# First attention of a two-block transformer: mask by a product on the scores, and the log of failure as a maximum

## What is computed

```
def stick_breaking_attention(q, k, v):
    scale = 1.0 / math.sqrt(d)
    for i in range(S // BLOCK):
        t0 = i * BLOCK
        kl = t0 + BLOCK
        z = jnp.einsum('bthd,bshd->bhts', q[:, t0:kl], k[:, :kl]).astype(jnp.float32) * scale
        mask = s_idx < t_idx
        log_fail = jnp.where(mask, jax.nn.log_sigmoid(-z), 0.0)
        later = lax.cumsum(log_fail, axis=3, reverse=True) - log_fail
        a = jnp.where(mask, jnp.exp(jax.nn.log_sigmoid(z) + later), 0.0)
        outs.append(jnp.einsum('bhts,bshd->bthd', a.astype(v.dtype), v[:, :kl]))
```

## Time and profile before

| | |
|---|---|
| median of 3 runs | 1379.29 us (1377.45 to 1379.47) |
| the profiled execution | 1380.28 us, its span 1378.5 us |
| PE matmul busy | 1083.2 us (79% of the span) |
| DVE busy | 480.4 us (35%) |
| ACT busy | 281.4 us (20%) |
| POOL busy | 56.9 us (4%) |
| DMA | 487.14 MB, 353 GB/s over the span |

### The profile page before, as it was taken

The page is one execution under the profiler, slowest core; times in us unless marked ns, Lnnn a source line. Parts: engine busy times, 40 slices in busy tenths (PEclk is TensorE's granted clock), DMA queues, the critical chain, the costliest instruction groups (busy, mean ns, idle before and its releaser), DMA issues.

```text
span 1378.5 us, 16712 instructions
## 1 busy us (share of the span) xinstructions
PE 1083.2 (79%) x7252; PEld 626.7 (45%) x7252; DVE 480.4 (35%) x900; ACT 281.4 (20%) x482; POOL 56.9 (4%) x83
## 2 busy tenths in 40 slices
PE   8999999999999997667684767667666675766766
PEld 7977886799977733132131312313133131312313
DVE  5977777897887311011010110101011010110113
ACT  6536665654254200000000000000000000000001
POOL 0005300000000000000000000000000000000000
PEclk9999999999999998787778887877787878888787
DMA  9755159444435999999999999999999999999995
GB/s 374 277 210 203 62 221 368 166 153 184 184 123 243 382 419 435 430 429 435 429 429 432 432 431 433 426 431 433 429 432 432 429 432 430 430 433 431 429 427 227
DMA packets 24672, 487.14 MB, mean 353 GB/s; under 512 B 2871, under 2 KB 4440, under 8 KB 5784
## 3 DMA queue, kind: packets, MB, share of 16 engines
q1 hardware_dynamic: 23480, 484.51, 83.6%
q10 hardware_dynamic: 1120, 1.57, 0.3%
HBM read 485.02 MB, written 1.05 MB: 353 GB/s over the span
## 4 chain that ended last, share of the span: by engine, by line
PE 68%; another core or an unknown queue 17%; DVE 8%; DMA 4%; issue 2%; ACT 1%; POOL 1%; DVEq 0%; SPq 0%; ACTq 0%
PE ps L284 66%; DMA pair<-in_expert_w 3%; DVE xT L1780 2%; DVE R L1748 1%; DVE R L1744 1%; DVE ring_r L338 1%; PE ps L1788 0%; DVE sm L1399 0%; DMA ring<-in_pieces 0%; POOL hT L796 0%; POOL hT L798 0%; DVE U_r L541 0%; PE ps L1422 0%; DVE hT L1413 0%
## 5 line engine op out<-in xcount | busy, mean ns | idle before, releaser
L284 PE MATMUL ps<-pair,R 128*32 128x512 f32 (+2 forms) x3168 | 485.5, 774 | 245.4 <-DMA pair<-in_expert_w 243.4
L284 PEld LDWEIGHTS ps<-pair,R 128*32 128x32 f32 x3168 | 116.2, 139 | 594.6 <-DMA pair<-in_expert_w 297.6
L284 PE MATMUL ps<-hT_r,ring_r 128*128 128x256 f32 x400 | 113.1, 283 | 0.0
L284 PE MATMUL ps<-U_r,ring_r 128*128 128x256 f32 x480 | 107.7, 284 | 0.4 <-DVE hT_r L529 0.3
L338 DVE TENSOR_TENSOR ring_r<-ring,ring_r 128x2048 fp32r<-128x2048 f32 (+1 forms) x44 | 98.7, 2275 | 23.8 <-ACT ring_r L332 23.6
L1744 DVE SCALAR_TENSOR_TENSOR R<-R,ps 128x512 f32<-128x512 f32 x16 | 11.0, 687 | 271.2 <-PE ps L284 271.2
L1741 DVE SCALAR_TENSOR_TENSOR R<-R,ps 128x512 f32<-128x512 f32 x16 | 11.0, 687 | 265.7 <-ACT R L1736 265.7
L284 PE MATMUL ps<-late_r,ring_r 128*128 128x256 f32 x448 | 84.4, 286 | 1.2 <-DVE U_r L541 0.9
L332 ACT ACTIVATE ring_r<-ring 128x2048 fp32r<-128x2048 f32 (+1 forms) x44 | 81.7, 1896 | 5.7 <-DMA ring<-in_pieces 5.7
L284 PEld LDWEIGHTS ps<-U_r,ring_r 128*128 128x128 f32 x480 | 82.1, 192 | 1.2 <-DVE hT_r L529 1.0
L1795 ACT ACTIVATE R<-ps 128x256 f32<-128x256 f32 x16 | 6.1, 383 | 363.5 <-PE ps L1788 363.5
(11 more groups left out here) (344 smaller groups left out, 1093.2 us busy)
## 6 DMA issues: line engine op xcount, KB each, us to landing
pair<-in_expert_w SPq DMA_DIRECT2D x87, 4096.0 KB, 52.8
ring<-in_pieces SPq DMA_DIRECT2D x20, 2048.0 KB, 8.4
pair<-in_expert_w SPq DMA_DIRECT2D x17, 2048.0 KB, 11.6
ring<-in_wmodt SPq DMA_DIRECT2D x8, 2048.0 KB, 8.2
ring<-in_wmodk SPq DMA_DIRECT2D x4, 2048.0 KB, 8.7
ring<-in_pieces SPq DMA_DIRECT2D x2, 1024.0 KB, 6.7
pair<-in_expert_w SPq DMA_DIRECT2D x2, 1024.0 KB, 41.9
ring<-in_pieces SPq DMA_DIRECT2D x1, 1792.0 KB, 11.8
```

What stands on the lines that cost most here:

```text
L284: mm = lambda e, o, l, r, st, sp_=True, sk=False: e.matmul(o, l, r, start=st, stop=sp_, skip_group_check=sk)
```

## The change

The mask is added to the scores by a product of `identb` with a bfloat16 tile `capb` (0 or -1e30), into the two diagonal pieces of the bank, right behind the scores. With the bank masked, L is worked out as max(z, ln(1 + exp(min(z, 30)))) in `sb_L`; DVE does the minimum and the maximum, ACT the exp and ln as before. The last exponential reads the bank directly. `pool_sb_z` and `dve_sb_c` are gone, and POOL has no part in the attention. `identb`, `causb` and the two halves of `capb` are filled by ACT before the attention, ahead of `act_filters(10)`. In DVE's loop `dve_sb_L` of pair i-1 stands behind `dve_sb_z` of pair i.

```diff
     def pe_sb_z(e, i):
         if i >= 3:
-            e.wait_ge(s["sb_min"], 2 * i - 4)
+            e.wait_ge(s["sb_a"], 2 * i - 4)
         elif i == 0:
             e.wait_ge(s["hf_a"], 7)
             e.wait_ge(s["rms_rt"], ROOTS[1])
+            e.wait_ge(s["b16"], 4)
...
         for h in hs:
-            k = mm(e, sb_b(h)[:, 256:384], k_[h][:, 128:256], q[h][:, 128:256], False, True, True)
+            mm(e, sb_b(h)[:, 256:384], k_[h][:, 128:256], q[h][:, 128:256], False, True, True)
+        for h in hs:
+            k = mm(e, sb_b(h)[:, 0:384].rearrange("p (a t) -> p a t", a=3)[:, 0:3:2, :], identb, capb, False, True, True)
         k.then_inc(s["sb_z"], 1)
 
     def dve_sb_z(e, h):
         e.wait_ge(s["sb_z"], h // 2 + 1)
+        if h >= 4:
+            e.wait_ge(s["sb_L"], h - 3)
+        elif h == 2:
+            e.wait_ge(s["gate"], 4)
+        e.tensor_scalar(sb_e1(h), sb_b(h)[:, 0:384], 30.0, None, ALU.min).then_inc(s["sb_mn"], 1)
+
+    def dve_sb_L(e, h):
+        e.wait_ge(s["sb_ln"], 2 * h + 2)
         if h >= 6:
             e.wait_ge(s["sb_c"], h - 5)
-        e.tensor_scalar(sb_L(h), sb_b(h)[:, 0:384], 0.0, None, ALU.max).then_inc(s["sb_mn"], 1)
-        e.wait_ge(s["sb_mn"], 2 * h + 1)
-        if h >= 4:
-            e.wait_ge(s["sb_L"], 2 * h - 7)
-        e.scalar_tensor_tensor(sb_e1(h), sb_b(h)[:, 0:384], 0.0, sb_L(h), ALU.min, ALU.subtract).then_inc(s["sb_mn"], 1)
+        e.tensor_tensor(sb_L(h), sb_e1(h), sb_b(h)[:, 0:384], ALU.max).then_inc(s["sb_L"], 1)
...
-    def dve_sb_c(e, h):
+    def act_sb_c(e, h):
         e.wait_ge(s["sb_c"], h + 1)
         if h >= 4:
             e.wait_ge(s["sb_o"], (h - 4) // 2 + 1)
-        e.tensor_tensor(sb_w(h), sb_b(h)[:, 0:384], c_("cap"), ALU.min).then_inc(s["sb_min"], 1)
-
-    def act_sb_c(e, h):
-        e.wait_ge(s["sb_min"], h + 1)
-        e.activation(sb_w(h), sb_w(h), ACT.Exp).then_inc(s["sb_a"], 1)
+        e.activation(sb_w(h), sb_b(h)[:, 0:384], ACT.Exp).then_inc(s["sb_a"], 1)
...
         conv(16)
+        e.activation(identb, c_("ident"), ACT.Copy).then_inc(s["b16"], 1)
+        e.activation(causb, c_("caus"), ACT.Copy).then_inc(s["b16"], 1)
+        for t in range(2):
+            e.activation(capb[:, t, :], c_("cap"), ACT.Copy).then_inc(s["b16"], 1)
         act_filters(e, 10)
...
         dve_sb_z(e, 2)
         dve_sb_z(e, 3)
+        dve_sb_L(e, 0)
+        dve_sb_L(e, 1)
         conv(18)
         for i in range(11):
-            if 0 <= i - 2 < 8:
-                dve_sb_c(e, 2 * i - 4)
-                if i == 9:
-                    dve_split_u(e, 2, 2, ac)
-                dve_sb_c(e, 2 * i - 3)
-                if i == 9:
-                    dve_split_u(e, 3, 3, ac)
-                    dve_split_u(e, 4, 4, ac)
             if 2 <= i < 8:
                 dve_sb_z(e, 2 * i)
                 dve_sb_z(e, 2 * i + 1)
+            if 2 <= i < 9:
+                dve_sb_L(e, 2 * i - 2)
+                dve_sb_L(e, 2 * i - 1)
+            if i == 9:
+                for c in (2, 3, 4):
+                    dve_split_u(e, c, c, ac)
             if 0 <= i - 3 < 8:
                 dve_sb_o(e, i - 3)
```

More of the change, by code:

```diff
@@ L43, in _const_layout @@
     at = 0
-    for name, n in [("nones", 128), ("ntri", 128), ("m01", 128),
-                    ("cap", 384), ("caus", 128), ("cosd", 128), ("sind", 128),
+    for name, n in [("nones", 128), ("ntri", 128),
+                    ("cap", 128), ("caus", 128), ("cosd", 128), ("sind", 128),
                     ("fwd", 1024), ("nyq", 256), ("inv", 1024)]:
@@ L66 @@
 l0_qk l0_v gate_r gate_t gate
-sb_z sb_mn sb_ln sb_L sb_c sb_min sb_a sb_o sb_u
+sb_z sb_mn sb_ln sb_L sb_c sb_a sb_o sb_u
 b16 lat st_a st_d lt_p lt_a pr_d
@@ L259, in _program @@
     identb, causb = b16[:, 0:128], b16[:, 128:256]
+    capb = b16[:, 256:512].rearrange("p (a t) -> p a t", a=2)
     KC = sb("KC", NKEPT)
@@ L777, in dve_sb_z @@
         e.wait_ge(s["sb_z"], h // 2 + 1)
+        if h >= 4:
[5 more added lines that the diff above has]
+        e.wait_ge(s["sb_ln"], 2 * h + 2)
         if h >= 6:
             e.wait_ge(s["sb_c"], h - 5)
-        e.tensor_scalar(sb_L(h), sb_b(h)[:, 0:384], 0.0, None, ALU.max).then_inc(s["sb_mn"], 1)
-        e.wait_ge(s["sb_mn"], 2 * h + 1)
-        if h >= 4:
-            e.wait_ge(s["sb_L"], 2 * h - 7)
-        e.scalar_tensor_tensor(sb_e1(h), sb_b(h)[:, 0:384], 0.0, sb_L(h), ALU.min, ALU.subtract).then_inc(s["sb_mn"], 1)
+        e.tensor_tensor(sb_L(h), sb_e1(h), sb_b(h)[:, 0:384], ALU.max).then_inc(s["sb_L"], 1)
     def act_sb_z(e, h):
-        e.wait_ge(s["sb_mn"], 2 * h + 2)
+        e.wait_ge(s["sb_mn"], h + 1)
         e.activation(sb_e1(h), sb_e1(h), ACT.Exp).then_inc(s["sb_ln"], 1)
@@ L790, in act_sb_z @@
         e.activation(sb_e1(h), sb_e1(h), ACT.Ln, bias=1.0).then_inc(s["sb_ln"], 1)
[L792 to L798, removed]
     def pe_sb_c(e, h):
         b, L = sb_b(h), sb_L(h)
-        e.wait_ge(s["sb_L"], 2 * h + 2)
+        e.wait_ge(s["sb_L"], h + 1)
         mm(e, b[:, 0:256], c_("ntri"), L[:, 0:256], False, True, True)
@@ L1980, in pe_program @@
                 if i == 9:
-                    e.wait_ge(s["sb_min"], 11)
+                    e.wait_ge(s["sb_a"], 11)
                     pe_proj(e, 16, cs=(0, 1), last=False, **XB)
@@ L2228, in act_program @@
         act_rms_root(e, 2)
-        e.activation(identb, c_("ident"), ACT.Copy).then_inc(s["b16"], 1)
-        e.activation(causb, c_("caus"), ACT.Copy).then_inc(s["b16"], 1)
         wait_col(e, 2)
@@ L2616, in pool_program @@
         e.memset(KB[0:1, 0, :], 0.0).then_inc(s["hf_z"], 1)
-        for h in range(16):
-            pool_sb_z(e, h)
         e.wait_ge(s["proj"], 30)
@@ L2660, in _constants @@
     c["ntri"] = -(p[:, None] >= p[None, :]).astype(f)
-    c["m01"] = (p[:, None] < p[None, :]).astype(f)
-    cap = np.where(p[:, None] < p[None, :], 0.0, NEG)
-    c["cap"] = np.concatenate([cap, np.zeros((128, 128)), cap], 1)
+    c["cap"] = np.where(p[:, None] < p[None, :], 0.0, NEG)
     c["caus"] = np.where(p[None, :] <= p[:, None], 0.0, NEG)
```

## The result

With the change the median of 20 runs is 1381.64 us (1378.87 to 1385.77), beside 1378.99 us (1375.67 to 1381.92) for 20 runs of the kernel before: a ratio of 1.0023, 95% interval 1.0015 to 1.0030, so 2.1 to 4.1 us slower. The forecast was +4.1 us and 1383.4 us. The profiled execution took 1384.91 us, its span 1383.1 us.

What follows compares the result with a forecast made beforehand. PE was taken to bound the first attention, whose delay moves the DMA-bound expert loads. Turns of 4.72 us make the loop 4.74 us late, less 0.66 in the tail: +4.1 us, 1383.4 us, range 1380.2 to 1386.5 (8 in 10).

Steps and rivals of the forecast that it cites:

- What bounds: First attention's loop before: PE works 3.61 us of a 4.01 us turn; the missing 0.40 us waits for POOL's masking.
- The ring: Attention loop: scores, two minima, first maximum, previous pair's cumulative products, next scores; 4.72 us a turn against 4.01.
- The mask product: On PE behind the scores: 0.25 us a pair of products, bounded by 0.21 and 0.70.
- Pair 0: First two heads of the loop: cumulative products at 122.61 instead of 122.11, after two pairs of mask products.
- pair 7: Last two heads of the loop, no minima in front: cumulative products at 153.58 instead of 148.84, 4.74 us late.
- The order of DVE's queue: Attention loop: two minima of pair i, waiting for its scores, stand ahead of pair i-1's two maxima.
- The tail: From pair 7's cumulative products to the last value products: 6.66 us instead of 7.32, giving back 0.66 us.
- What was to cost nothing: Four ACT copies, 0.31 us each, in 2.99 us of idle before an eviction; last exponential reading the bank.
- The delay swallowed: Rival: 2.3 us of PE waits between 157.9 and 384 us vanish, leaving +1.8 us, 1381.1 us; chance 0.12.
- The DVE rule of the Trainium skill: Minima and maximum in the loop: about 1.64 us by the rule, 1.55 by the rows, which the forecast used.
- The clock: Rival: PE's clock falls to 1.2 GHz in the attention, 7.7 us a turn, about +18 us, 1401 us; chance 0.03.
- The total: Whole kernel: 4.74 us late at pair 7 less 0.66 us in the tail, +4.1 us, 1383.4 us; chance 0.68.

Runs made afterwards that it cites:

- before without POOL's multiplication: Kernel before, with POOL's multiplication by the 0/1 mask left out of the computation: turn 3.61 us, attention 49.14 us against 52.49 before.
- maxima first: Changed kernel with DVE's two maxima of pair i-1 queued ahead of the minima of pair i: median 1375.55 us, ratio to before 0.9986.
- alternating: Changed kernel with DVE's queue ordered minimum, maximum, minimum, maximum: turn 4.36 us, attention 54.07 us against 52.49 before.
- without mask product: Changed kernel with the mask of the diagonal pieces left out of the computation: turn 4.45 us, attention 54.48 us against 52.49 before.
- POOL masks: Changed kernel with maxima ahead of minima, no mask product on PE, POOL multiplying by the 0/1 mask: median 1375.10 us, ratio to before 0.9981.
- the repeat: Changed kernel once more, no edit: median 1382.71 us in 5 runs, ratio to before 1.0038 (1.0025 to 1.0052).

## Why the prediction was right, point by point

- **What bounds.** As said: PE full but for 0.40 us a turn in the mean, and that was POOL ("before without POOL's multiplication": 3.61 us).
- **The ring.** 4.72 us forecast, 4.77 measured. Its terms: 1.95 us of cumulative products was 133.67 - 131.71 = 1.96; 0.97 + 0.25 us to the first minimum was 134.95 - 133.67 = 1.28; the three DVE operations and the hand-over were 136.49 - 134.95 = 1.54, forecast 1.55. PE's wait was to be some 0.9 us and is 0.77, or 4.77 - 3.93 = 0.84 from start to start.
- **The mask product.** Mis-sized both ways: 0.25 us a pair forecast, 0.32 in the loop, and 0.16 instead of 0.50 us for the two pairs between projections. Pair 0 stood 0.34 us earlier than forecast (122.27, not 122.61), and from there to pair 7 it took 0.33 us more (31.30, not 30.97). That pair 7 stood at 153.57 where 153.58 was written is luck: the two errors cancelled.
- **The order of DVE's queue.** Nothing was taken or added in "maxima first", and 6.06 us of 56.54 went. With the order as in the change, "alternating" and "without mask product" took off what the ring says.
- **The tail.** 160.20 - 153.57 = 6.63 us, forecast 6.66, against 7.32: the splits took 0.4 us each. All six traces in which POOL has no part show 6.62 to 6.64 us; the three in which it works show 7.32, 7.01 (without its multiplication) and 6.91 ("POOL masks").
- **What was to cost nothing.** ACT's idle before the last eviction ahead of the scores shrank from 2.99 to 2.19 us, and the first scores started at 103.66 as before. The last exponential takes 0.49 us from the bank, 0.52 from S.
- **The delay swallowed.** The rival fell: the first expert load moved by 4.45 us, 4.04 of it the attention. In seven of the nine traces it follows the last value products by 227.77 to 227.81 us, wherever these stand, so nothing of the shift is lost on the way; the change (228.18) and "alternating" (227.98) have a little more, see the end. For "maxima first" it moved by -2.77: -2.01 of attention and -0.78 of an earlier start.
- **The DVE rule of the Trainium skill** ("VectorE: DVE Perf Modes", the TRN2 errata and "The DRAIN you can't avoid"), as the prediction applied it, would have made the three operations 1.64 us, as an estimate. The measured 1.54 decides, and two independent minima took 1.02 us together, not twice 0.55. The prediction left out half of that section: it adds that a next operation that isn't held starts earlier, and these rows agree.
- **The clock.** The granted clock stayed 1.00 in the attention with PE busy 83% of it. The short idles between groups, of which the Trainium skill ("TensorE: Matmul & The Clock Gate", "A second HAM failure mode: psum-queue depth-cycling") warns, brought no throttling here.
- **The total.** +4.1 us forecast, 4.05 in the attention, and 3.2 us by the ratio (2.1 to 4.1). Whether the true total is 3.2 or 4.05 stays open: the interval holds both, only just in the second case, and the repeat's (3.4 to 7.2 us) holds 4.05 and not 3.2. By the total alone the swallowed delay (+1.8 us, a ratio of 1.0013) would be only just outside the interval; it is the trace that rules it out.

## What to carry to other kernels

When work moves from one engine to another, its duration is the smaller part: ask what it queues behind. Here DVE was busy for 11.89 of 28.00 us in the attention, before for 22.49, and yet it is what PE now waited for. An operation whose inputs are long ready must not stand behind one that waits for the very engine that wants its result; here the same instructions, with two lines of the loop exchanged, turn +4.05 into -2.01 us. And an engine that is 90% full can give back at most the other 10%, so work put on it is dear: the mask products cost 2.06 us with the ring, where they stand in the chain ahead of the minima, and 0.32 us a turn without it (3.93 us in "maxima first", 3.61 in "POOL masks").

## What the runs showed that I had not expected

- The time from the first expert load to the end of the span is not fixed, although the DMA engines run without a gap (share 1.00): 1378.5 - 383.93 = 994.57 us before, 994.72 with the change, but 991.15 in its repeat and 1375.5 - 385.03 = 990.47 in "alternating". The other five traces lie between. These 4 us between executions are as large as the change, and most likely the greater part of the scatter of the totals (6.9 us over the 20 runs of the change); only the profiled executions show them. What makes them is open.
- In the profiled execution of the change one load of 2 MB in front of the latent attention took 8.75 us, and is on the chain that ended last:

```profile
192.21 8.75 DMA ring<-in_pieces
200.98 1.92 ACT ring_r L333
202.92 4.50 DVE ring_r L339 x2
209.49 18.23 PE ps L285 x116
```
```profile
209.49 5.75 PE L285 MATMUL ps<-ring,R 128*128 128x384 f32 x17 [0.42 <-ACT R L927]
```
In the kernel before PE goes from 201.01 through without this wait. In the changed kernel's PE timeline it costs 0.42 us at 209.49, which is the rest of the 4.45. In seven of the nine traces, the repeat's among them, ACT begins to convert what this load brings (L332 before, L333 with the change) 8.37 or 8.38 us after the load is issued, in the change's 200.98 - 192.21 = 8.77 us, in "alternating" 8.56. So it looks like a thing of the execution and not of the change.
- A bfloat16 product of 256 columns costs 0.04 to 0.16 us apiece by what stands around it: 0.16 for two pairs (four products) between projections, 0.32 for one pair (two products) in the loop, 0.22 for a second pair behind the first. Why the first ones between projections are so cheap is open.
